# ScalarE in place of GpSimd issues the key copies of the last two attention jobs, and VectorE splits one downward tile sooner

## The chip, the cores and the metric

The program runs on one core of one Trainium2 chip. The metric is device microseconds of one execution (us), lower is better. The kernel before was timed three times: 1089.26, 1090.0 and 1090.44 us, median 1090.0.

PE is TensorE, DVE is VectorE, ACT is ScalarE, POOL is GpSimd and SP is SyncE, which issues the loads. Times inside the profiled execution are us from the start of its span.

## What is computed

One layer of a streaming encoder, batch 1, 512 positions, width 1024, in float32. With `cond = silu(c)` and nine vectors of shift, scale and gate from `cond @ w_ada + b_ada`:

```
h = modulate(x, g_ffn1, shift0, scale0); x = x + 0.5*gate0*swiglu(h, w_ffn1_up, w_ffn1_down)
h = modulate(x, g_mix, shift1, scale1);  proj = h @ w_in     # 8 stick-breaking + 8 forgetting heads of 64
o_sb = rmsnorm(stick_breaking_attention(sb_q, sb_k, sb_v))
o_fx = rmsnorm(forgetting_attention(rmsnorm(fx_q), rmsnorm(fx_k), fx_v, cumsum(log_f))) * sigmoid(fox_gate)
x = x + gate1 * (concat(o_sb, o_fx) @ w_out)
h = modulate(x, g_ffn2, shift2, scale2); x = x + 0.5*gate2*swiglu(h, w_ffn2_up, w_ffn2_down)
return rmsnorm(x, g_final)
```

`swiglu(h, u, d)` is `(silu(gate) * up) @ d`, with gate and up the two halves of `h @ u`; the hidden width is 2816.

## The kernel before

**Products of two halves.** Every float32 operand of a product is kept as a high part in the rounded type float32r and a low part, the rest. A product is three passes on PE (lines 887 to 889, in `three`): high by high, high by low, low by high. So each weight tile of 128x1024 that SP loads (line 763) goes through two steps before PE may use it: ACT writes its high part, DVE subtracts it to get the low part. SP may load the tile that is four later only when DVE has done the low part of the tile in that slot (`load_w` waits on `w_lo_done`).

**Attention jobs.** The 16 heads are worked on in pairs, as eight jobs: 0 to 3 are stick-breaking, 4 to 7 forgetting heads. A job has five units of scores, numbered 0 to 4 below. The order of all work of this stage is one list, `STEPS`, which `mixer_steps` writes in Python from a pattern of letters, some lags and a few steps moved by hand (`AHEAD`). Each engine walks through the same list and does its own share of every step, so an engine never overtakes the list. The steps named below:

- `scores(j, u)`: PE multiplies queries by `k_hh` (line 1194) and `k_l` (line 1195) and adds a mask (line 1196).
- `prep(j, u)`: for forgetting heads DVE subtracts the decay and takes the maximum (line 2415) and negates it (line 2421), then ACT takes the exponential (line 1787). `sum` is DVE's scaling (lines 2444, 2448).
- `turn(j, u)`: PE transposes (line 1218). `unload(j, u)`: ACT copies the high part `pt_hi` (line 1801), DVE subtracts to `pt_lo` (line 2455). `values(j, h)`: PE multiplies by v.
- `square`, `stat`, `scale`, `part`: the norm of a q, k or output chunk. `square` is ACT's line 1730, `stat` PE's line 1246 and ACT's lines 1737 and 1739, `scale` DVE's 2367 and 2372. `part` of a k writes `k_hh` on ACT (line 1757, two halves of 64 partitions) and `k_l` on DVE (line 2390).
- `decay(j, h)`: PE's line 1255 and ACT's line 1765. `evac` of a gate chunk: DVE copies it out (line 2344), ACT takes its sigmoid in three passes (lines 1702, 1704, 1706).

**The copies of k.** Scores need the high part of k on both halves of the partitions. After `part` has written the two halves of `k_hh[j % 2]`, POOL copies each to the other 64 partitions with a DMA from SBUF to SBUF (`repeat_k`, lines 673 and 675, 128 KB each). They count up `k_twice[j % 2]`, and `scores(j, 0)` on PE waits for it. Then POOL issues the next pieces of a set of weight sums that it makes in DRAM for the second FFN (`one_piece`, lines 701 and 703, 1280 KB each, one in flight at a time). SP reads them when the second FFN begins (line 850).

In the list around jobs 6 and 7 the order is:

```
split(93) part(k6) unload(5,2) scores(5,4) prep(5,4) decay(6,0) ... values(5,0) ... decay(6,1) unload(5,3)
scores(6,0) stat(11) prep(6,0) turn(5,4) prep(6,1) scale sum(6,0) unload(5,4) part(q7) scores(6,1) proj turn(6,0) values(5,1)
split(95) part(k7) unload(6,2) scores(6,4) prep(6,4) decay(7,0) ... values(6,0) evac(g6) ... decay(7,1) unload(6,3)
scores(7,0) prep(7,0) ... scores(7,1) ... values(6,1) evac(g7) square(14) ... unload(7,0) scores(7,2) stat(14)
```

**From the up half to the down half of the second FFN.** The hidden chunks (22 of 128x512) are split into high (ACT, line 1522) and low parts (DVE, line 2066, `hidden2_low`). The down weights come in tiles of two chunks of rows, except the third and fourth, which have one each:

```
NAT_PARTS = ((0, 2), (2, 2), (4, 1), (5, 1)) + tuple((k, 2) for k in range(6, 22, 2))
```

A tile passes DVE (`gated`, line 1922, times the gate), ACT (`split_down`, line 1421, high part) and DVE (`split_down_lo`, line 1929, low part). ACT may write the high part of tile n only when PE has finished tile n - 2, since there are two buffers. PE then does tile after tile in order. The order on DVE is written out by hand: low parts of hidden chunks 4 and 5, `gated` of tiles 2 and 3 (counted from 0), chunks 6 to 16, `gated` of tile 4, chunks 17 to 21, and then in turn low part of tile 2, `gated` 5, low part of tile 3, `gated` 6, low part of tile 4, `gated` 7, and so on. Chunk 4 is all that tile 2 (the third) multiplies.

Of the kernel before, what the change touches and what calls it, by code (L numbers as in the profile page):

```python
# [7 lines left out]
F32 = mybir.dt.float32  # L8
# [5 lines left out]
P = 128  # L14
# [6 lines left out]
HD = 64  # L21
# [24 lines left out]
T_DOWN2 = T_UP2 + 2 * SEVEN0 + 4 * (FC - SEVEN0)  # L46
# [5 lines left out]
SPLIT = 2  # L52
# [248 lines left out]
def hybrid_block_kernel(  # L301
# [4 lines left out]
    with ctx:  # L306
        def sem(name):
            return ctx.enter_context(nc.semaphore(name))
# [14 lines left out]
        def keep(name, shape, dt=F32):  # L323
# [103 lines left out]
        k_hh, k_l = (k_hh_a, k_hh_b), (k_l_a, k_l_b)  # L427
# [53 lines left out]
        silu_done, hid_f32, hid_hi_done, hid_done = (  # L481
            sem("silu_done"), sem("hid_f32"), sem("hid_hi_done"), sem("hid_done"))
        mix_zero, k_zero = sem("mix_zero"), sem("k_zero")
        k_twice = [sem("k_twice0"), sem("k_twice1")]
        wf_split, wf_split_hi, f_logit, f_sum, f_act, f_dve = (
            sem("wf_split"), sem("wf_split_hi"), sem("f_logit"), sem("f_sum"), sem("f_act"), sem("f_dve"))
# [154 lines left out]
        def _(pool):  # L641
# [28 lines left out]
            def repeat_k(j):  # L670

                pool.wait_ge(*k_made(j))
                g.dma_start(k_hh[j % 2][HD:P, 0, :].bitcast(F32), k_hh[j % 2][0:HD, 0, :].bitcast(F32))\
                    .then_inc(k_twice[j % 2], 16)
                g.dma_start(k_hh[j % 2][0:HD, 1, :].bitcast(F32), k_hh[j % 2][HD:P, 1, :].bitcast(F32))\
                    .then_inc(k_twice[j % 2], 16)
# [59 lines left out]
                if n == 0:  # L736
                    repeat_k(0)
            for j in range(1, JOBS):
                repeat_k(j)
                if j in (1, 2):  # L740
                    for r in (2 * j - 2, 2 * j - 1):
                        one_piece(sums_rows(S1, r), pieces_rows(up_b, r), True)
                    one_piece(sums_rows(S4, j + 1), pieces_rows(gate_b, j + 1), False)
                elif j == 3:
                    for r in range(3):
                        one_piece(sums_rows(S3, r), pieces_rows(up_a, r), True)
                elif j == 4:
                    one_piece(sums_rows(S3, 3), pieces_rows(up_a, 3), True)
                    one_piece(sums_rows(S2, 0), sums_rows(S1, 0), True)
                elif j == 5:  # L750
                    for r in range(1, 4):
                        one_piece(sums_rows(S2, r), sums_rows(S1, r), True)
                else:
                    for r in (2 * j - 12, 2 * j - 11):
                        one_piece(sums_rows(S4, r), sums_rows(S2, r), True)
# [126 lines left out]
        def _(pe):  # L882
# [167 lines left out]
            for n in range(KC - 1):  # L1050
                pe.wait_ge(x_upd, n + KC - 1)
                for part, (k0, nk) in enumerate(DOWN_PARTS):
                    t = T_DOWN1 + 3 * n + part
# [7 lines left out]
            n = KC - 1  # L1061
            side_bank = (bank[1][:, 0:HALF], bank[3][:, 0:HALF])
            pe.wait_ge(x_upd, n + KC - 1)
            t = T_DOWN1 + 3 * n
# [61 lines left out]
            for step in STEPS:  # L1126
# [49 lines left out]
                elif kind == "scores":  # L1176
                    _, j, u = step
                    unit = 5 * j + u
                    if u == 0:

                        if j == 0:
                            pe.wait_ge(k_zero, 4)
                        pe.wait_ge(k_twice[j % 2], 32 * (j // 2 + 1))
                        if j < SBJ:
                            pe.wait_ge(qk_ready, 2 * j + 2)
                        else:
                            pe.wait_ge(nrm_lo, norm_of("k", j) + 1)
# [210 lines left out]
        def _(act):  # L1398
# [266 lines left out]
            for step in STEPS:  # L1665
# [53 lines left out]
                elif kind == "square":  # L1719
                    m = step[1]  # L1720
                    what, n, ci = NORMS[m]
                    if what == "o":
                        act.wait_ge(pv_done, 2 * n + 2)
                    else:
                        act.wait_ge(w_used, CHUNKS[ci][3] + 1)
                    if m:
                        act.wait_ge(stat_done, stats)
                    else:
                        act.wait_ge(f_dve, 4)
                    a(ssum[:], bank[6 if what == "o" else CHUNKS[ci][2]][:], ACT.Square).then_inc(nsq_done, 1)  # L1730
                elif kind == "stat":
                    m = step[1]
                    stats += 1
                    act.wait_ge(stat_done, stats)
                    if m:
                        act.wait_ge(nrm_f32, m)
                    a(rstd[:], bank[7][:], ACT.Ln, bias=EPS).then_inc(stat_read, 1)
                    act.wait_ge(stat_read, stats)
                    a(rstd[:], rstd[:], ACT.Exp, scale=-0.5).then_inc(nrstd_done, 1)
                elif kind == "part":  # L1740
                    m = step[1]
                    what, n, ci = NORMS[m]
                    if what == "o":
                        if n >= SBJ:
                            act.wait_ge(nrm_gated, n - SBJ + 1)
                        else:
                            act.wait_ge(nrm_f32, m + 1)
                        a(o_hi[:, n, :], nrm[:], ACT.Copy, scale=col(R_GO + n)).then_inc(nrm_hi, 1)
                    else:
                        act.wait_ge(nrm_f32, m + 1)  # L1750
                        act.wait_ge(s_done, 5 * (n - 1))
                        for h in range(2):
                            rows = slice(h * HD, (h + 1) * HD)
                            if what == "q":
                                last = a(q_st[rows, n % 2, h, :], nrm[rows, :], ACT.Copy, scale=gq8[rows, :])
                            else:
                                last = a(k_hh[n % 2][rows, h, :], nrm[rows, :], ACT.Copy, scale=col(R_GK)[rows, :])
                        last.then_inc(nrm_hi, 1)
                elif kind == "decay":
                    _, j, h = step  # L1760
                    stats += 1
                    act.wait_ge(stat_done, stats)
                    if j > SBJ:
                        act.wait_ge(*z_read(5 * j - 1))
                    a(f_keys[:, h, :], bank[7][:], ACT.Copy).then_inc(stat_read, 1)
                elif kind == "prep" and step[1] < SBJ:

                    unit = 5 * step[1] + step[2]
                    buf = tmp_a[:, unit % 2, :]
                    act.wait_ge(s_done, unit + 1)  # L1770
                    if unit >= 2:
                        act.wait_ge(scan_done, unit - 1)
                    a(buf, bank[2 + unit % 2][:], ACT.Abs).then_inc(abs_done, 1)
                    act.wait_ge(abs_done, unit + 1)
                    a(buf, buf, ACT.Exp, scale=-1.0).then_inc(eneg_done, 1)
                    act.wait_ge(eneg_done, unit + 1)
                    a(buf, buf, ACT.Ln, bias=1.0).then_inc(e_ready, 1)
                elif kind == "prep":

                    _, j, u = step  # L1780
                    unit = 5 * j + u
                    buf = tmp_b[:, unit % 2, :]
                    fx = unit - 5 * SBJ
                    act.wait_ge(zf_ready, fx + 1)
                    for s, (h, i, c0) in enumerate(UNITS[u]):
                        seg = buf[:, c0:c0 + (i + 1) * P]
                        last = a(seg, seg, ACT.Exp, bias=small[:, 4 * (unit % 2) + s:4 * (unit % 2) + s + 1],
                                 accum_out=small[:, 8 + 4 * (unit % 2) + s:9 + 4 * (unit % 2) + s])
                    last.then_inc(exp_done, 1)
                elif kind == "exp" and step[1] < SBJ:  # L1790
                    unit = 5 * step[1] + step[2]
                    act.wait_ge(d_ready, unit + 1)
                    a(tmp_b[:, unit % 2, :], tmp_b[:, unit % 2, :], ACT.Exp).then_inc(p_ready_sb, 1)
                elif kind == "unload":
                    _, j, u = step
                    unit = 5 * j + u
                    act.wait_ge(t_done, unit + 1)
                    for h, dst, src in turned(u):
                        if j:
                            act.wait_ge(pv_done, 2 * (j - 1) + h + 1)  # L1800
                        last = a(pt_hi[:, h, dst, :], blocks(bank[4 + unit % 2], src), ACT.Copy)
                    last.then_inc(pt_hi_done, 1)
# [101 lines left out]
        def _(dve):  # L1904
# [654 lines left out]
            for chunk in range(4, FC):  # L2559
                hidden2_low(chunk)  # L2560
                if chunk == 5:
                    gated(2)
                    gated(3)
                elif chunk == 16:
                    gated(4)

            for t in range(T_DOWN2 + SPLIT, T_DOWN2 + len(NAT_PARTS) + SPLIT):
                split_down_lo(t)
                gated(t - T_DOWN2 + 3)
            for tb in range(TB):  # L2570

# [39 lines left out]
```

## Time and profile before

| what | value |
|---|---|
| median of 3 runs | 1090.0 us |
| the profiled execution's own time | 1089.68 us |
| its span in the trace | 1087.9 us |
| granted clock of TensorE | 0.999 of full speed |
| PE busy | 1070.9 us, 98% of the span |
| DVE, ACT, POOL busy | 64%, 46%, 4% |
| chain that ended last | PE 89%, DVE 4%, DMA 2%, ACT 2%, issue 1% |

The span is the time from the first to the last record of the trace; the execution's own time holds 1.8 us around it. PEld is the loading of weights into TensorE, ahead of the matmul that uses them. In a row of a timeline the number in brackets is how long the engine was idle before the row, and the arrow names what it waited for. The first number is the start, the second the duration of all that the row holds.

### The profile page before, as it was taken

How to read it: one execution, taken by the hardware profiler on the slowest of the kernel's cores; microseconds unless marked ns; L12 is line 12 of the kernel's file. 1: busy time of each engine (PE TensorE's matmuls, PEld its weight loads, DVE VectorE, ACT ScalarE, POOL GpSimd, SP SyncE). 2: the span in 40 equal slices, each digit the busy share in tenths (PEclk: the TensorE clock that was granted, in tenths of full speed). 3: DMA queues.
4: the chain of work that ended last, by engine and by line, in shares of the span. 5: the costliest groups of instructions: out<-in, count | busy, mean ns of one | idle time of the engine just before them, and what ended most of it. 6: DMA issues, size and time to landing. Idle time of an engine off the chain costs nothing.

```text
span 1087.9 us, 16282 instructions
## 1 busy us (share of the span) xinstructions
PE 1070.9 (98%) x6072; PEld 911.4 (84%) x6072; DVE 691.8 (64%) x1054; ACT 500.9 (46%) x833; POOL 42.3 (4%) x76
## 2 busy tenths in 40 slices
PE   8999999999999999999999999999999999999997
PEld 5788888888878889888778777789999999978886
DVE  3755555555653557886786676678766667684343
ACT  5523222223222235776796776358544454541222
POOL 1000000000000001110111011000000000000000
PEclk9999999999999999999999999999999999999999
DMA  9868888885474552398699567246777667132221
GB/s 344 239 211 292 264 276 283 275 306 156 140 228 130 176 157 79 90 221 203 142 187 197 124 145 165 77 125 156 190 200 193 171 181 203 60 106 98 87 97 78
DMA packets 209053, 191.84 MB, mean 176 GB/s; under 512 B 7660, under 2 KB 183900, under 8 KB 206940
## 3 DMA queue, kind: packets, MB, share of 16 engines
q1 hardware_dynamic: 201392, 146.86, 45.8%
q0 software_dynamic: 7424, 44.04, 16.1%
q8 instruction: 42, 0.69, 0.3%
q14 instruction: 23, 0.19, 0.1%
q10 hardware_dynamic: 172, 0.06, 0.0%
HBM read 186.74 MB, written 44.04 MB: 212 GB/s over the span
## 4 chain that ended last, share of the span: by engine, by line
PE 89%; DVE 4%; DMA 2%; ACT 2%; issue 1%; SPq 0%; DVEq 0%; POOL 0%; ACTq 0%
PE bank L887 27%; PE bank L889 27%; PE bank L888 27%; PE bank L1246 1%; PE bank L898 1%; PE bank L1218 1%; DVE hid_lo L2066 1%; PE bank L1194 1%; PE bank L1195 1%; DMA x_nat<-in_x_dram 1%; DMA k_hh_b<-k_hh_b 0%; PE bank L924 0%; ACT w_hi L1411 0%; DMA k_hh_a<-k_hh_a 0%; DVE y L2584 0%
## 5 line engine op out<-in xcount | busy, mean ns | idle before, releaser
L887 PE MATMUL bank<-h_hi,w_hi 128*128 128x512 f32 (+1 forms) x592 | 230.3, 389 | 0.1
L889 PE MATMUL bank<-h_hi,w_lo 128*128 128x512 f32 (+1 forms) x592 | 223.5, 378 | 0.0
L888 PE MATMUL bank<-h_lo,w_hi 128*128 128x512 f32 (+1 forms) x592 | 223.5, 378 | 0.0
L1912 DVE TENSOR_TENSOR w_lo<-w_raw,w_hi 128x1024 fp32r<-128x1024 f32 x97 | 118.7, 1225 | 156.1 <-ACT w_hi L1411 155.5
L1411 ACT ACTIVATE w_hi<-w_raw 128x1024 fp32r<-128x1024 f32 x97 | 102.5, 1058 | 204.0 <-PE bank L889 179.2
L887 PEld LDWEIGHTS bank<-h_hi,w_hi 128*128 128x128 f32 x592 | 111.8, 189 | 25.5 <-issue 4.2
L888 PEld LDWEIGHTS bank<-h_lo,w_hi 128*128 128x128 f32 x592 | 111.7, 189 | 24.0 <-issue 2.9
L889 PEld LDWEIGHTS bank<-h_hi,w_lo 128*128 128x128 f32 x592 | 111.6, 189 | 22.6
L2018 DVE TENSOR_TENSOR up_lo<-up_raw,up_hi 128x1024 fp32r<-128x1024 f32 x80 | 86.6, 1085 | 21.1 <-ACT up_hi L1480 21.1
L889 PE MATMUL bank<-combo,up_lo 128*128 128x256 f32 x320 | 90.6, 283 | 0.0
L887 PE MATMUL bank<-combo,up_hi 128*128 128x256 f32 x320 | 90.6, 283 | 0.0
L888 PE MATMUL bank<-combo,up_hi 128*128 128x256 f32 x320 | 90.2, 282 | 0.0
L1480 ACT ACTIVATE up_hi<-up_raw 128x1024 fp32r<-128x1024 f32 x80 | 75.2, 943 | 0.0
L887 PE MATMUL bank<-hid_hi,w_hi 128*128 128x512 f32 (+1 forms) x198 | 74.0, 374 | 1.0 <-DVE w_lo L1912 1.0
L889 PE MATMUL bank<-hid_hi,w_lo 128*128 128x512 f32 (+1 forms) x198 | 73.5, 371 | 0.0
L888 PE MATMUL bank<-hid_lo,w_hi 128*128 128x512 f32 (+1 forms) x198 | 73.4, 371 | 0.0
L889 PE MATMUL bank<-w_hi,hid_lo 128*128 128x512 f32 x176 | 69.8, 396 | 0.0
L887 PE MATMUL bank<-h_hi,up_hi 128*128 128x256 f32 x240 | 68.0, 283 | 0.0
L888 PE MATMUL bank<-h_lo,up_hi 128*128 128x256 f32 x240 | 67.7, 282 | 0.0
L889 PE MATMUL bank<-h_hi,up_lo 128*128 128x256 f32 x240 | 67.6, 282 | 0.0
L1421 ACT ACTIVATE w_hi<-down_raw 128x1024 fp32r<-128x1024 f32 (+1 forms) x24 | 23.7, 987 | 86.6 <-PE bank L889 82.0
L1941 DVE SCALAR_TENSOR_TENSOR ada_acc<-ada_w,cond,ada_acc 128x1024 f32<-128x1024 f32 x49 | 62.6, 1278 | 0.0
(274 smaller groups left out, 2173.5 us busy)
## 6 DMA issues: line engine op xcount, KB each, us to landing
w_sums<-in_w_ffn_up_dram POOLq DMA_DIRECT2D x24, 1280.0 KB, 8.9
ada_w<-in_w_ada_dram SPq DMA_DIRECT2D x56, 512.0 KB, 3.8
w_raw<-in_w_ffn_up_dram SPq DMA_DIRECT2D x48, 512.0 KB, 7.2
up_raw<-w_sums SPq DMA_DIRECT2D x40, 512.0 KB, 5.5
w_raw<-in_w_in_dram SPq DMA_DIRECT2D x28, 512.0 KB, 3.8
w_sums<-w_sums POOLq DMA_DIRECT2D x8, 1280.0 KB, 10.3
up_raw<-in_w_ffn_up_dram SPq DMA_DIRECT2D x20, 512.0 KB, 4.1
down_raw<-in_w_ffn_down_dram SPq DMA_DIRECT2D x20, 512.0 KB, 3.7
```

What stands on the lines that cost most here:

```text
L887: mm(dst, wh, xh, start=start, stop=False, skip_group_check=skip)
L888: mm(dst, wh, xl, start=False, stop=False, skip_group_check=skip)
L889: return mm(dst, wl, xh, start=False, stop=stop, skip_group_check=skip)
L898: last = mm(bank[4 + p][:], cond[:, k:k + 1].broadcast_to([P, P]), ada_first[:, p, k, :], start=k == 0, stop=k == KC - 1)
L1194: mm(zb[:, c0:c0 + n], qs, k_hh[j % 2][:, h, 0:n], start=True, stop=False)
L1195: mm(zb[:, c0:c0 + n], qs, k_l[j % 2][:, h, 0:n], start=False, stop=False)
L1411: a(w_hi[:, s, :], w_raw[:, r, :], ACT.Copy).then_inc(w_hi_done, 1)
L1421: a(w_hi[:, t % SPLIT, 0:n], down_raw[:, t % RAW, 0:n], ACT.Copy).then_inc(w_hi_done, 1)
L1480: a(up_hi[f % 2][q][:], up_raw[n % 3][q][:], ACT.Copy).then_inc(w_hi_done, 1)
L1912: v.tensor_tensor(w_lo[:, s, :], w_raw[:, r, :], w_hi[:, s, :].bitcast(F32), ALU.subtract)\
L1941: ins = v.scalar_tensor_tensor(ada_acc[:], source, cond[:, k:k + 1], ada_acc[:], ALU.mult, ALU.add)
L2018: v.tensor_tensor(up_lo[s][q][:], up_raw[s][q][:], up_hi[f % 2][q][:].bitcast(F32), ALU.subtract)\
```

## The change

Copies of k for jobs 6 and 7 are issued by ACT, right behind the ACT instructions that write `k_hh`, after a wait for their completion. They count up new semaphores, `k_again`, for which PE waits in those jobs. POOL no longer issues them; at its place in these two jobs it waits until they have landed, before it issues the next pieces of the sums. And on DVE the low part of down tile 2 is made after hidden chunk 11 instead of after chunk 21.

```diff
+        k_again = [sem("k_again0"), sem("k_again1")]
...
             for j in range(1, JOBS):
-                repeat_k(j)
+                if j < 6:
+                    repeat_k(j)
+                else:
+                    pool.wait_ge(k_again[j % 2], 32)
...
-                        pe.wait_ge(k_twice[j % 2], 32 * (j // 2 + 1))
+                        pe.wait_ge(*((k_twice[j % 2], 32 * (j // 2 + 1)) if j < 6 else (k_again[j % 2], 32)))
...
                         last.then_inc(nrm_hi, 1)
+                        if what == "k" and n >= 6:
+                            act.wait_ge(*k_made(n))
+                            act.dma_start(k_hh[n % 2][HD:P, 0, :].bitcast(F32), k_hh[n % 2][0:HD, 0, :].bitcast(F32))\
+                                .then_inc(k_again[n % 2], 16)
+                            act.dma_start(k_hh[n % 2][0:HD, 1, :].bitcast(F32), k_hh[n % 2][HD:P, 1, :].bitcast(F32))\
+                                .then_inc(k_again[n % 2], 16)
...
                 if chunk == 5:
                     gated(2)
                     gated(3)
+                elif chunk == 11:
+                    split_down_lo(T_DOWN2 + SPLIT)
                 elif chunk == 16:
                     gated(4)
 
             for t in range(T_DOWN2 + SPLIT, T_DOWN2 + len(NAT_PARTS) + SPLIT):
-                split_down_lo(t)
+                if t > T_DOWN2 + SPLIT:
+                    split_down_lo(t)
                 gated(t - T_DOWN2 + 3)
```

## Rows read from the trace of the kernel before

**Rows 1.** Waits of PE over the whole span: total us, times, longest.
```profile
PE bank L887 <- DVE w_lo L1929: 1.6, 2, 1.3
PE bank L1194 <- DMA k_hh_b<-k_hh_b: 1.3, 1, 1.3
PE bank L1194 <- DMA k_hh_a<-k_hh_a: 1.0, 1, 1.0
```

**Rows 2.** Timeline of all engines around the copies of job 6: start, us, engine.
```profile
626.89 0.66 ACT L1801 ACTIVATE pt_hi<-bank 128x256 fp32r<-128x256 f32 x2
626.90 1.51 DVE L2390 SCALAR_TENSOR_TENSOR k_l_a<-nrm,vcol,k_hh_a 64x512 fp32r<-64x512 f32 x2
...
627.16 0.57 POOL L673 DMA_DIRECT2D k_hh_a<-k_hh_a  x1 [21.56 <-ACT k_hh_a L1757]
...
627.71 0.54 POOL L675 DMA_DIRECT2D k_hh_a<-k_hh_a  x1
...
628.44 0.76 DVE L2455 TENSOR_TENSOR pt_lo<-bank,pt_hi 128x256 fp32r<-128x256 f32 x2
...
632.88 0.49 PE L1194 MATMUL bank<-k_hh_a,q_st 128*128 128x512 f32 x1 [1.01 <-DMA k_hh_a<-k_hh_a]
```

**Rows 3.** Chain of waits, jobs 6 and 7: start and length of the second copy.
```profile
627.71 5.12 DMA k_hh_a<-k_hh_a
...
653.82 5.38 DMA k_hh_b<-k_hh_b
```

**Rows 4.** Timeline: DMA issues of ACT at the start, one of SP beside job 6.
```profile
1.04 0.59 ACTq L1427 DMA_DIRECT2D vecs<-in_c_dram  x1
1.67 0.34 ACTq L1427 DMA_DIRECT2D vecs<-in_b_ada_dram  x1
```
```profile
626.97 0.38 SPq L763 DMA_DIRECT2D w_raw<-in_w_out_dram  x1
```

**Rows 5.** DMA issues, windows 434 to 436 and 553 to 555: median us to landing.
```profile
k_hh_a<-k_hh_a POOLq DMA_DIRECT2D x2, 128.0 KB, 2.5
```
```profile
k_hh_a<-k_hh_a POOLq DMA_DIRECT2D x2, 128.0 KB, 8.9
```

**Rows 6.** Timelines of POOL and SP: last piece of the sums, first reads of them.
```profile
666.64 0.88 POOL L701 DMA_DIRECT2D w_sums<-w_sums  x1 [11.30 <-DMA w_sums<-w_sums]
```
```profile
725.62 1.66 SPq L850 DMA_DIRECT2D up_raw<-w_sums  x2
```

**Rows 7.** Timeline behind scores(6,0).
```profile
634.59 0.68 DVE L2415 CUSTOM_DVE_ANT_0 tmp_b<-bank,f_keys 128x512 f32<-128x512 f32 x1
...
635.79 0.56 DVE L2415 CUSTOM_DVE_ANT_0 tmp_b<-bank,f_keys 128x384 f32<-128x384 f32 x1 [0.32 <-PE bank L1196]
...
639.16 0.19 PEld L887 LDWEIGHTS bank<-pt_hi,v_hi 128*128 128x128 f32 x1 [0.35 <-DVE pt_lo L2455]
```

**Rows 8.** Timeline of PE and ACT behind scores(7,0).
```profile
659.25 0.50 PE L1194 MATMUL bank<-k_hh_b,q_st 128*128 128x512 f32 x1 [1.27 <-DMA k_hh_b<-k_hh_b]
```
```profile
667.76 0.64 ACT L1702 ACTIVATE sig<-sig 128x512 f32<-128x512 f32 x1 [0.65 <-DVE sig L2344]
...
669.63 0.58 ACT L1730 ACTIVATE ssum<-bank 128x512 f32<-128x512 f32 x1
```

**Rows 9.** Timelines of DVE, ACT and PE at the first down tiles.
```profile
957.66 6.70 DVE L2066 TENSOR_TENSOR hid_lo<-hid,hid_hi_b 128x512 fp32r<-128x512 f32 x11
...
968.43 0.68 DVE L1929 TENSOR_TENSOR w_lo<-down_raw,w_hi 128x512 fp32r<-128x512 f32 x1
...
972.95 1.22 DVE L1922 TENSOR_TENSOR down_raw<-down_raw,tmp_b 128x1024 f32<-128x1024 f32 x1 [2.11 <-DMA down_raw<-in_w_ffn_down_dram]
```
```profile
962.38 0.63 ACT L1421 ACTIVATE w_hi<-down_raw 128x512 fp32r<-128x512 f32 x1 [2.30 <-PE bank L889]
```
```profile
969.16 0.50 PE L887 MATMUL bank<-w_hi,hid_hi_b 128*128 128x512 f32 x1 [1.27 <-DVE w_lo L1929]
...
975.37 0.50 PE L887 MATMUL bank<-w_hi,hid_hi_b 128*128 128x512 f32 x1 [0.34 <-DVE w_lo L1929]
```

## The prediction

> **What bounds the kernel now.** PE does. I read the page first: PE is busy 98% of the span and makes up 89% of the chain that ended last, so only a wait of PE is worth anything. The second view is therefore the list of PE's waits [rows 1]. Two of its entries are the copies of k for jobs 6 and 7, 1.0 and 1.3 us, and one is the low part of down tiles, 1.6 us in two waits. The two edits aim at these: 3.9 us at most, 0.36% of the time. The third view is the timeline around each wait, to see what stands right behind it; there most of the 3.9 us goes again. About 0.2% (2.2 us) is what a measurement of this kernel can tell from no change.
>
> **Copies of k: when they can start.** ACT has written k_hh at 626.87, just before its next instruction starts at 626.89; POOL's first issue starts only at 627.16 and its second at 627.71 [rows 2]. ACT can start at about 626.95 (0.05 us for the wait on its own result, my guess from the 0.02 to 0.05 us between dependent rows). How long ACT takes to issue a DMA is shown only at the start of the kernel: 0.34 us for 72 rows, 0.59 us for the first of all [rows 4]. The copies have 64 rows each, so I take 0.34. The second copy is then issued at 627.3 instead of 627.71, 0.4 us sooner, and the same in job 7.
>
> **When they land.** Before, the second copy took 5.12 and 5.38 us [rows 3]. The same copy from POOL took 2.5 us in job 0, with nothing beside it, and 8.9 us in job 4 [rows 5]. Those are the bounds. The nearest rows are those of jobs 6 and 7 themselves: SP issues a load of w_out at 626.97, beside the copies [rows 4], and still will. What goes is POOL's 0.54 us of issue, against ACT's 0.34 [rows 2, 4], and the piece of the sums that POOL issued behind the copies, because POOL now waits for them. I take 4.7 us: landing at 632.0 instead of 632.83, and some 1.1 us sooner in job 7 (4.7 against 5.38, and 0.4 from the start). The Trainium skill, page DMA: Bandwidth & Descriptors, section Issuing engines are not separate DMA queues, says that all issuing engines feed the same 16 DMA engines and another one saves only sequencer time. By that the landing would be only 0.4 us sooner in each job, and the gain below 0.3 + 0.4 instead of 0.3 + 0.65 us; no run so far shows such a copy from ACT.
>
> **What ACT pays.** Behind the copies ACT has unload(5,2), its pt_hi at 626.89 for 0.66 us, done at 627.55. DVE takes it up only at 628.44, since k_l holds DVE from 626.90 to 628.41 [rows 2]. So pt_hi may be 0.86 us late for nothing. The two issues and the wait are 0.05 + 2 x 0.34, and about 0.05 to get going: 0.8 us. I count 0.05 us per job. By the long issue of rows 4 it would be 0.1 + 2 x 0.59 = 1.3 us, so 0.4 us late per job. After pt_hi ACT waits for DVE for about 2.5 us, so nothing else of ACT is touched.
>
> **What POOL pays.** In job 6 its piece goes out about 3 us later, and so do the pieces behind it. The last was issued at 666.64, and SP's first read of the sums is at 725.62 [rows 6]. Nearly 50 us cover it, less the roughly 10 us that a piece takes. Cost 0.
>
> **What is late next, job 6.** PE's 1.01 us before scores(6,0) can go. But DVE's prep(6,0) at 634.59 starts with no wait on PE, since DVE and ACT are behind with their own work, and it won't move. Only prep(6,1), which waited 0.32 us for PE's scores, can come sooner [rows 7]. Its exponential on ACT, then pt_hi and pt_lo of unload(5,4) and PE's values(5,1) at 639.16 hang on it; there PE already waited 0.35 us for DVE [rows 7]. So PE, 1 us ahead, waits there about 0.7 us longer: of 1.01 us, 0.32 stay.
>
> **Job 7.** PE's 1.27 us go [rows 8]. Behind it ACT's and DVE's preps again run on their own time. ACT waits 0.65 us for the gate copy that DVE makes once PE is done with it, then does three passes for the sigmoid and square(14) at 669.63, without a gap [rows 8]. PE's stat(14) waits for that square. ACT's work before the 0.65 us does not move, so square(14) and with it PE can come at most 0.65 us sooner. Of 1.27, 0.65 stay. Sum of the copies: -0.32 - 0.65 + 2 x 0.05 = -0.87 us.
>
> **The down tile.** From 957.66 DVE does chunk after chunk at 6.70 / 11 = 0.61 us, 0.60 from start to start. Chunk 11 is the sixth of this row, so its end is 957.66 + 6 x 0.60 = 961.27. But ACT's high part of tile 2 is there only at 962.38 + 0.63 = 963.01, because it waits for PE to finish tile 0 [rows 9]. DVE, put there, stands still for 1.75 us, with the ten other chunks, gated 4 and 5 and the low part of tile 3 queued behind. The low part of tile 2 is then done at 963.7, and PE's wait of 1.27 us goes: it starts tile 2 at 967.9 instead of 969.16. But DVE ends chunk 21 at 968.43 + 1.75 + 0.60 = 970.8 and needs 1.13 for gated 5 and 0.68 for the low part of tile 3, to 972.6. Tiles 2 and 3 took PE from 969.16 to 975.37 - 0.34 = 975.03, so 2.94 each. PE is through tile 2 at 970.85, waits 1.8 us, starts tile 3 at 972.65 and is through at 975.6. Tile 4 started at 975.37 before. DVE does gated 6 (its load is now there 5 us sooner, so the 2.11 us wait for the DMA goes) and the low part of tile 4 by 972.5 + 1.15 + 1.2 = 974.9 (both steps at the 1.22 us of the 1024-wide row), in time. PE starts tile 4 at 975.6: **0.2 us later than before**. The wait is moved, not removed. Bounds: nothing from these rows could make it better than the 1.61 us of both waits; for the worse, another 0.3 us if DVE is a little slower.
>
> **Sum.** -0.87 + 0.2 = -0.7 us. The profiled execution took 1089.68 us, 1.8 more than its span, 0.3 less than the median of 1090.0; against the median I get 1089.3.
>
> **The rivals.** (a) *PE keeps all that it wins at the copies*: -1.01 - 1.27 + 0.2 = -2.1, so 1087.9. For it: the waits are PE's own, on the chain. Against: the two later waits named above stand in the rows, 0.35 and 0.65 us [rows 7, 8]. (b) *Both edits give in full*: -3.9, so 1086.1. It needs DVE not to stand still at chunk 11, against the 963.01 of rows 9. (c) *ACT issues slowly*, at 0.59 us each: SP issues its load at the same moment [rows 4], and if ACT has to wait for SP, pt_hi is 0.4 us late per job, the whole row of DVE and ACT work behind it too, and the gain of the copies shrinks from 0.97 to 0.2: 1090.0. The Trainium skill, page Perfetto Trace Analysis, section DMA Instruction — HWDGE (DVE, Sync), says that the descriptor generator is shared between sequencers and locked for exclusive use, which speaks for (c). Against (c): at the start of the kernel SP was issuing too, and ACT's second DMA already took only 0.34 us [rows 4]. (d) *The copies land later than before*: it decides from 5.5 us after ACT's second issue on (632.83 - 627.3). The mechanism is the load of w_out, which now goes out at the same moment as the copies and may be served first. At 6.8 us, half way between 4.7 and the 8.9 of job 4 [rows 5], PE waits 1.3 us longer per job: +2.6 + 0.2, so 1092.8. Against: job 4 had a piece of the sums in flight ahead of the copies in the same queue, and here the queue of ACT is empty. (e) *The change of the issuing engine does nothing for PE*, since the landing hangs on the load alone: only the +0.2 of the down tile is left, 1090.2.
>
> **How the numbers follow.** My forecast 0.56; (a) 0.11, (b) 0.04, (c) 0.14, (d) 0.06, (e) 0.09. The forecast, (c) and (e) lie within 0.2% of 1090.0 (1087.8 to 1092.2), (a) just inside, and I give half of it to the other side. Faster by over 0.2%: (b) and half of (a), 0.10. Slower: (d), 0.05. Within: 0.85. For the range I take in (a) at the low end, 1087.7, and (c) and (e) at the high end with the 0.4 us by which runs of one kernel lie above their median, 1090.7. Left out are (b), (d) and the tails, about 0.17.
>
> **What would show it.** In the changed profile: two DMA rows on ACT's queue behind k_hh, 0.3 to 0.4 us each; no wait of PE at line 1194; but a longer wait at values(5,1) for pt_lo, near 1 us, and a new one of 0.6 us at stat(14) for ACT's square. At the down tiles DVE idle for 1.7 us before the low part of tile 2, for ACT; PE's 1.27 us before tile 2 gone and 1.8 us before tile 3 in its place; the 0.34 us before tile 4 gone. I am wrong if PE still waits at line 1194, if ACT's issues are 0.6 us, or if PE starts tile 3 without a wait.

## The result, and the profile after the change

The changed kernel takes **1091.67 us** (median of 20 runs, 1090.17 to 1093.11), the kernel before on the same chip 1089.67 us (20 runs, 1088.66 to 1092.51). The ratio is 1.0013, with a 95% interval of 1.0007 to 1.0019: slower, but by less than the 0.2% that the prediction took as telling a change from none. The 1089.3 us of the prediction and its range up to 1090.7 missed. The profiled execution took 1092.31 us: span 1090.5, granted clock 0.997 (before: 1087.9 and 0.999).

The waits of PE in the changed kernel (total us, times, longest), to be held against [rows 1]. PE's and ACT's lines are 4 further down than before, DVE's 10.

```profile
PE bank L891 <- DVE w_lo L1939: 2.0, 1, 2.0
PE bank L891 <- DVE w_lo L1922: 1.4, 2, 0.9
PE bank L891 <- DVE pt_lo L2465: 0.9, 2, 0.6
...
PE bank L1198 <- DMA k_hh_b<-k_hh_b: 0.5, 1, 0.5
PE bank L1250 <- ACT f_keys L1775: 0.4, 1, 0.4
...
PE bank L1198 <- DMA k_hh_a<-k_hh_a: 0.3, 1, 0.3
```

The waits on the copies did shrink, from 1.0 and 1.3 us to 0.3 and 0.5. In their place stand two waits for `pt_lo`, the low part of the transposed block (0.9 us), and one for `f_keys` (0.4). The down tiles have one wait of 2.0 us instead of two of 1.6 in all. All of PE's waits in this view make 10.5 us, against 10.0 before, only 0.5 us more; a list of waits does not show at what clock PE works. That is the second half of the loss, below.

The timeline of the changed kernel around the copies of job 6, against [rows 2, 4]:

```profile
627.05 0.53 ACTq L1765 DMA_DIRECT2D k_hh_a<-k_hh_a  x1
...
627.12 0.39 SPq L767 DMA_DIRECT2D w_raw<-in_w_out_dram  x1
...
627.61 0.88 ACTq L1767 DMA_DIRECT2D k_hh_a<-k_hh_a  x1
...
628.59 0.66 ACT L1811 ACTIVATE pt_hi<-bank 128x256 fp32r<-128x256 f32 x2 [1.57 <-issue]
...
629.28 0.76 DVE L2465 TENSOR_TENSOR pt_lo<-bank,pt_hi 128x256 fp32r<-128x256 f32 x2 [0.72 <-ACT pt_hi L1811]
...
630.09 0.50 PE L891 MATMUL bank<-pt_hi,v_hi 128*128 128x512 f32 x1 [0.34 <-DVE pt_lo L2465]
```

ACT issues for 0.53 and 0.88 us, in job 7 for 0.49 and 1.14, where I had taken 0.34 each. ACT does no work for 1.57 us ahead of `pt_hi`, and DVE, which was to find it ready, stands still for 0.72 us. The chain of waits of the changed kernel goes the same way (start, us, what):

```profile
627.05 0.53 ACTq L1765
627.61 0.88 ACTq L1767
628.59 0.67 ACT pt_hi L1811 x2
...
629.62 0.41 DVE pt_lo L2465
...
631.68 0.49 ACT f_keys L1775
```
```profile
654.25 5.82 DMA k_hh_b<-k_hh_b
```

In job 6 the chain does not pass through a copy at all: it is ACT's two issues, then PT, then `f_keys`. In job 7 it is the copy again, 5.82 us against the 5.38 of [rows 3].

Now the down tiles, in the timelines of DVE, ACT and PE, against [rows 9]:

```profile
963.99 0.69 DVE L1939 TENSOR_TENSOR w_lo<-down_raw,w_hi 128x512 fp32r<-128x512 f32 x1 [1.70 <-ACT w_hi L1425]
...
972.89 0.69 DVE L1939 TENSOR_TENSOR w_lo<-down_raw,w_hi 128x512 fp32r<-128x512 f32 x1
```
```profile
963.32 0.63 ACT L1425 ACTIVATE w_hi<-down_raw 128x512 fp32r<-128x512 f32 x1 [2.30 <-PE bank L893]
```
```profile
973.63 0.50 PE L891 MATMUL bank<-w_hi,hid_hi_b 128*128 128x512 f32 x1 [2.00 <-DVE w_lo L1939]
973.97 0.40 PE L892 MATMUL bank<-w_lo,hid_hi_b 128*128 128x512 f32 x1
...
975.69 0.63 PE L892 MATMUL bank<-w_lo,hid_hi_b 128*128 128x512 f32 x1
976.12 0.63 PE L893 MATMUL bank<-w_hi,hid_lo 128*128 128x512 f32 x1
```

The waits are the forecast ones: DVE stands still for 1.70 us, and PE's wait is moved from before tile 2 to before tile 3. But then the matmuls change their pace, from one each 0.23 to 0.24 us to one each 0.43. The windows of this stretch say why. A row has start and end, its length, the busy time of PE, PEld, DVE, ACT and POOL with the number of instructions, then the granted clock, the DMA share and GB/s:

```profile
972.00:973.50 1.50, 0.00 (x0) 0.00 (x0) 1.50 (x3) 0.78 (x1) 0.00 (x0) 1.00 0.00 0
973.50:975.00 1.50, 1.37 (x6) 1.14 (x7) 1.50 (x3) 0.00 (x0) 0.00 (x0) 0.99 0.14 30
975.00:976.50 1.50, 1.50 (x5) 1.16 (x4) 0.84 (x1) 0.00 (x0) 0.00 (x0) 0.50 0.78 294
976.50:978.00 1.50, 1.50 (x5) 1.16 (x4) 0.71 (x1) 0.00 (x0) 0.00 (x0) 0.50 0.55 191
978.00:979.50 1.50, 1.50 (x8) 1.17 (x7) 0.81 (x2) 1.06 (x1) 0.00 (x0) 0.87 0.49 184
```

PE is idle, works for 1.4 us at full clock, and is then granted **half of it, 1.2 instead of 2.4 GHz, for 3.4 us**. In the profile before, the clock was 1.00 all through this stretch, as in this row around tile 4:

```profile
975.00:976.50 1.50, 1.16 (x6) 0.95 (x6) 1.31 (x2) 1.06 (x1) 0.00 (x0) 1.00 0.02 1
```

Summed over the windows of the changed kernel, 1.7 us of full clock are missing.

PE's starts, before and after, give the account. The matmul of `f_cum` ahead of job 6 starts at 625.87 and 626.03, the output projection's first waiting matmul at 701.88 and 702.78: the copies cost 0.74 us. Tile 2 starts at 969.16 and 968.66, tile 3 at 972.06 and 973.63, tile 4 at 975.37 and 977.82: 1.55 us lost behind 701.88, and 0.2 more by the time the clock is back. Before the copies the two traces are 0.16 apart. So 0.2 + 0.7 + 1.7 make the 2.6 us between the spans.

### The profile page after: what moved, and what is told of

Its sections match the earlier page's. It is cut to its first block, busy times and chain, and to the rows that moved or that the text cites. A ratio compares the mean times of both kernels' runs of the same rounds, so it can differ in the third digit from the quotient of the medians.

```text
span 1090.5 us, 16284 instructions
## 1 busy us (share of the span) xinstructions
PE 1073.0 (98%) x6072; PEld 912.4 (84%) x6072; DVE 692.2 (63%) x1054; ACT 500.9 (46%) x833; POOL 40.0 (4%) x72
## 4 chain that ended last, share of the span: by engine, by line
PE 89%; DVE 4%; ACT 3%; DMA 2%; issue 1%; ACTq 0%; SPq 0%; DVEq 0%
PE bank L891 27%; PE bank L893 27%; PE bank L892 27%; PE bank L1250 1%; PE bank L902 1%; PE bank L1222 1%; PE bank L1198 1%; DMA w_raw<-in_w_ffn_down_dram 1%; PE bank L1199 1%; DMA x_nat<-in_x_dram 1%; PE bank L1285 1%; ACT w_hi L1415 1%; DMA k_hh_b<-k_hh_b 1%; DVE hid_lo L2076 1%; PE bank L928 0%
```

## The experiments

Twelve kernels ran in three groups (e1 to e4, e5 to e8, e9 to e12), each on another chip. So each ratio is against the kernel before on its own chip. Beside times I read two stretches of each profile, from starts of the same matmuls of PE: **jobs 6 and 7** (`f_cum` at 625.87 to the output projection at 701.88, 76.01 us before), and **down tiles** (from there to tile 4 at 975.37, 273.49 us before). The ratio is not the quotient of the two medians beside it; the two differ by up to 0.11% (e5: 1.0009 by the medians).

| kernel | median, its chip's before | ratio, 95% interval | jobs 6, 7 | down tiles |
|---|---|---|---|---|
| before | | | 76.01 | 273.49 |
| the change | 1091.67, 1089.67 | 1.0013 (1.0007-1.0019) | 76.75 | 275.04 |
| e1 copies only | 1091.19, 1090.85 | 1.0000 (0.9989-1.0010) | 76.80 | 273.49 |
| e2 tile only | 1092.25, 1090.85 | 1.0005 (0.9995-1.0015) | 78.00 | 275.12 |
| e3 tile at chunk 16 | 1088.90, 1090.85 | 0.9979 (0.9970-0.9988) | 76.50 | 271.92 |
| e4 GpSimd copies, SP holds | 1089.87, 1090.85 | 0.9987 (0.9979-0.9996) | 75.13 | 273.83 |
| e5 ACT copies, SP just behind | 1090.82, 1089.82 | 1.0020 (1.0010-1.0030) | 76.17 | 273.83 |
| e6 ACT copies, SP holds | 1090.48, 1089.82 | 1.0008 (1.0000-1.0017) | 76.16 | 273.86 |
| e7 ACT copies late | 1090.35, 1089.82 | 0.9999 (0.9991-1.0008) | 75.75 | 273.50 |
| e8 e4 and e3 | 1087.23, 1089.82 | 0.9976 (0.9966-0.9986) | 75.16 | 271.94 |
| e9 tile at chunk 13 | 1089.03, 1090.91 | 0.9990 (0.9981-1.0000) | 75.76 | 272.54 |
| e10 the change, tile at 16 | 1089.00, 1090.91 | 0.9985 (0.9975-0.9994) | 76.53 | 271.97 |
| e11 as e2 | 1092.14, 1090.91 | 1.0007 (0.9996-1.0018) | 76.59 | 275.29 |
| e12 as e4 | 1089.83, 1090.91 | 0.9995 (0.9986-1.0004) | 75.17 | 273.75 |

### The two edits apart

**e1** has the change's edits of the copies, without the line on DVE; **e2** has only that line. **e3** has it at another place, behind chunk 16 and its pieces:

```diff
                 elif chunk == 16:
                     gated(4)
+                    split_down_lo(T_DOWN2 + SPLIT)
```
**e4** leaves the copies with POOL and holds SP's two loads of w_out beside them until the copies have landed:

```diff
-            with sp.Fori(0, KC // RAW) as i:
-                for j in range(RAW):
-                    load_w(T_OUT + RAW * i + j, j, tile8(w_raw, j), out_v[:, :, bass.ds((RAW * i + j) * P, P)])
+            for n in range(KC):
+                if n == 1:
+                    sp.wait_ge(w_lo_done, T_OUT + n - RAW + 1)
+                    sp.wait_ge(k_twice[0], 128)
+                if n == 3:
+                    sp.wait_ge(w_lo_done, T_OUT + n - RAW + 1)
+                    sp.wait_ge(k_twice[1], 128)
+                load_w(T_OUT + n, n % RAW, tile8(w_raw, n % RAW), out_v[:, :, n * P:(n + 1) * P])
```

> The copies of k for jobs 6 and 7 from ACT, the down tile as before. Theory A (ACT's issues are long, and pt_hi behind them is late): as in the changed kernel, pt_hi of unload(5,2) and unload(6,2) starts about 1.6 us after k_hh, PE waits 0.3 to 0.6 us for pt_lo and still 0.3 to 0.5 us for the copies, and everything after attention is 0.7 us later than before: +0.7 us. No drop of the granted clock near the down tiles, and PE waits 1.27 and 0.34 us there as before. Rival: the copies are worth the forecast -0.9 us and the whole loss is in the down tiles; then this run is 0.9 us below before.

> Only the down tile's low part after chunk 11, the copies on POOL as before. Theory B (the standstill of DVE makes one PE wait of 2.0 us, and behind it the granted clock halves for some 3.3 us): PE starts tile 3 about 0.6 us later than before and is 1.5 us slower in the stretch after it, so up to +1.8 us where the clock falls and +0.2 us where it doesn't; runs lie in two groups 1.6 us apart. Rival: the clock fell in that profile for another reason and has nothing to do with the wait; then this run is +0.2 us with the clock at 1.00 throughout.

> The low part of down tile 2 after hidden chunk 16 and gated 4, where ACT's high part (963.0) has long been there, the copies as before. If the order on DVE alone is what failed: DVE does not stand still, PE starts tile 2 at 967.9 instead of 969.2, tile 3 and tile 4 without a wait, the clock stays at 1.00: -1.5 us against before (1.27 + 0.34 less restarts). Rival (PE's waits there are set by loads or the order of later steps and only move): -0.2 to +0.2 us, with a wait of PE before tile 3 or 4 of over 1 us.

> POOL issues the copies as before, but SP holds the w_out loads of tiles 97 and 99, which went out beside them, until the copies of jobs 6 and 7 have landed. Theory C (the load beside them is what makes the copies take 5.1 and 5.4 us): they land in about 2.6 us as in job 0, PE's waits at the copies go, and by the limits behind them (0.32 and 0.65 us) the kernel is 0.9 to 1.0 us faster. Rival (the piece of the sums behind them, or the path of the copies itself): landing stays at 4.4 us or more, change within 0.3 us of before.

Measured: the copies alone lengthen jobs 6 and 7 to 76.80 us, as the whole change does. The tile alone gives PE's 2.00 us wait before tile 3, half clock behind it, and the slow down tiles of the whole change. So by these stretches both edits lose, and each does it without the other. The times alone do not show it: the median of e2 is 1.4 us above its chip's, that of e1 0.3 us, and neither is clear of no change by its interval.

e3 keeps the idea of the tile and takes the standstill out. Its timeline of DVE:

```profile
960.13 6.70 DVE L2066 TENSOR_TENSOR hid_lo<-hid,hid_hi_b 128x512 fp32r<-128x512 f32 x11
966.76 1.22 DVE L1922 TENSOR_TENSOR down_raw<-down_raw,tmp_b 128x1024 f32<-128x1024 f32 x1
967.89 0.68 DVE L1929 TENSOR_TENSOR w_lo<-down_raw,w_hi 128x512 fp32r<-128x512 f32 x1
968.50 3.09 DVE L2066 TENSOR_TENSOR hid_lo<-hid,hid_hi_b 128x512 fp32r<-128x512 f32 x5
```

DVE never waits for ACT, since `w_hi` is long there at 967.89, and the low part is still done before PE wants it. Both PE waits of [rows 9] are gone (one of 0.2 us is left, before tile 3), the down tiles take 1.6 us less, and the time falls by 0.2%.

e4 shows what the copies are bound by. With SP's load held, PE has no wait on a copy. Jobs 6 and 7 take 75.13 us, 0.88 us less than before and not 2.3, because PE now waits for ACT a little later, once in each job:

```profile
635.77 0.67 PE L1251 MATMUL bank<-ssum,pair_mean 128*128 128x512 f32 x1 [0.98 <-ACT f_keys L1770]
```
```profile
671.77 1.12 PE L1251 MATMUL bank<-ssum,pair_mean 128*128 128x512 f32 x2 [0.79 <-ACT ssum L1735]
```

The first is stat(11), right behind scores(6,0): of PE's 1.0 us in job 6 it leaves 0.1. The second is stat(14), which waits for ACT's square: of job 7's 1.3 us it leaves about 0.65, the limit that the prediction had named.

In the four kernels that hold SP's loads and leave the tile alone (e4, e5, e6, e12) the down tiles take 0.3 to 0.4 us longer than before. It is lost ahead of tile 4, where PE waits 0.55 to 0.69 us (e4, e6, e12) instead of 0.34, and DVE ahead of it 2.33 to 2.46 us for a load of the down weights instead of 2.11. No run separates why.

### Why ACT's copies lose: the issues or the landing

**e5** and **e6** leave the copies with ACT and hold SP's load, e5 only until ACT has done the unload behind its two issues (`sp.wait_ge(pt_hi_done, 28)` and 33), e6 until the copies have landed (`k_again`, 32). **e7** moves ACT's two issues behind `pt_hi` of unload(5,2) and unload(6,2):

```diff
                         last = a(pt_hi[:, h, dst, :], blocks(bank[4 + unit % 2], src), ACT.Copy)
                     last.then_inc(pt_hi_done, 1)
+                    if (j, u) in ((5, 2), (6, 2)):
+                        n = j + 1
+                        act.wait_ge(*k_made(n))
+                        act.dma_start(k_hh[n % 2][HD:P, 0, :].bitcast(F32), k_hh[n % 2][0:HD, 0, :].bitcast(F32))\
+                            .then_inc(k_again[n % 2], 16)
+                        act.dma_start(k_hh[n % 2][0:HD, 1, :].bitcast(F32), k_hh[n % 2][HD:P, 1, :].bitcast(F32))\
+                            .then_inc(k_again[n % 2], 16)
```

> ACT issues the copies for jobs 6 and 7, and the output projection's tile that SP loads beside them (two of them, one per job) is held on SP until ACT has finished the unload that follows its two issues. Theory 1 (ACT's issues are long, 0.53 and 0.88 us for job 6, 0.49 and 1.14 us for job 7, because SP's load of many descriptors is issued at the same moment and shares what makes them): each of the four issues takes 0.35 to 0.5 us, PT's unload starts 0.6 to 0.9 us sooner than with the change, the copies land under 4 us after their issue, and the values matmul group before TensorE's new scores loses no 0.3 us. Theory 2 (the length belongs to an SBUF to SBUF copy issued from ACT): 0.5 and 0.9 to 1.1 us as before, only the landing gets shorter. Time by theory 1 about 1 us below the kernel before, by theory 2 at most 0.5 us below.

> As the run before it, but SP holds its load until both copies of the job have landed, so nothing of SP's lies beside the copies at all. Both theories: landing 2 to 3.5 us after the issue, no wait of TensorE on a copy. Theory 1 (issue length from SP's simultaneous load): issues 0.35 to 0.5 us, the time is that of the kernel in which GpSimd copies and SP holds its load (0.9987 of before), less or more by 0.3 us. Theory 2 (intrinsic length): issues still 0.5 and 0.9 to 1.1 us and TensorE still loses 0.3 to 0.6 us per job on PT's unload, so slower than that kernel by about 1 us.

> ACT issues the copies only after the unload of the last PT unit of the job before (about 0.7 us later than with the change), SP's loads as in the kernel before. If what costs with the change is that the issues stand ahead of PT's unload on ACT, the idle time of ACT ahead of that unload falls from 1.6 to 1.8 us to under 0.7 us, TensorE's values group no longer waits 0.34 to 0.56 us on PT's low part, and the copies land 0.7 to 1.5 us later, so TensorE's wait on them grows from 0.33 and 0.49 us to 1 to 1.6 us: time within 0.5 us of the kernel before. The rival, that the copies are late whoever issues them and wherever, gives the same wait on the copies as the kernel before, 1.0 to 1.7 us, and the same time.

> GpSimd copies, SP holds its load until they have landed: once more, against the kernel in which ACT issues the copies and SP holds as well (1.0008 on another chip, this one 0.9987 on a third). TensorE's times between jobs 5 and 8 showed 0.4 us lost in job 6 and 0.6 us in job 7 by ACT's issues alone, so this kernel should stand about 1 us under that one: 0.9985 to 0.9995. If it is 1.0005 or above, ACT's issues cost nothing and the difference was the chip's.

The timeline of e6 around job 6, where nothing of SP's is issued beside ACT:

```profile
628.24 0.52 ACTq L1770 DMA_DIRECT2D k_hh_a<-k_hh_a  x1
...
628.79 0.60 ACTq L1772 DMA_DIRECT2D k_hh_a<-k_hh_a  x1
...
629.50 0.66 ACT L1816 ACTIVATE pt_hi<-bank 128x256 fp32r<-128x256 f32 x2 [1.29 <-issue]
...
630.19 0.76 DVE L2470 TENSOR_TENSOR pt_lo<-bank,pt_hi 128x256 fp32r<-128x256 f32 x2 [0.44 <-ACT pt_hi L1816]
```

and the same place in e12, where POOL issues:

```profile
627.70 0.66 ACT L1806 ACTIVATE pt_hi<-bank 128x256 fp32r<-128x256 f32 x2
...
627.97 0.57 POOL L673 DMA_DIRECT2D k_hh_a<-k_hh_a  x1 [21.42 <-ACT k_hh_a L1762]
...
628.53 0.54 POOL L675 DMA_DIRECT2D k_hh_a<-k_hh_a  x1
...
629.25 0.76 DVE L2460 TENSOR_TENSOR pt_lo<-bank,pt_hi 128x256 fp32r<-128x256 f32 x2
```

My theory 1, that SP's load makes ACT's issues long, falls for the most part. Without it they take 0.52 and 0.60 us in job 6 and 0.47 and 0.84 in job 7 (e5: 0.60 and 0.88). With it, the second took 0.63 to 0.88 in job 6 (e1, e10 and the change) and 0.87 to 1.20 in job 7, and in e7 0.99 and 0.82, so the load adds 0 to 0.4 us, to the second issue only. That is all the sharing that the Trainium skill's page Perfetto Trace Analysis (section DMA Instruction — HWDGE (DVE, Sync), a descriptor generator locked for exclusive use) could account for here.

The landing is another matter. The views of the DMA issues, job 7 of e6 and of the change (median us to landing; job 6 has 2.3 and 5.1):

```profile
k_hh_b<-k_hh_b ACTq DMA_DIRECT2D x2, 128.0 KB, 2.4
```
```profile
k_hh_b<-k_hh_b ACTq DMA_DIRECT2D x2, 128.0 KB, 5.3
```

The load beside them costs the copies nearly 3 us, whoever issues them (POOL's medians are 4.8 and 4.9 us before, 2.6 and 2.4 in e4). ACT writes `k_hh` 0.16 us later than before in job 6 and 0.73 us later in job 7. Counted from there, it issued the second copy 0.3 us sooner than POOL had, and PE started on it at 633.05 - 0.16 = 632.89 and 660.11 - 0.73 = 659.38, against 632.88 and 659.25 before: **nothing was won**. That is what the Trainium skill's page DMA: Bandwidth & Descriptors, section Issuing engines are not separate DMA queues, leads to (the same 16 DMA engines serve all), and less than I had made of it.

What ACT's issues cost by themselves can be read from the stretch of jobs 6 and 7 in the five kernels in which no copy is late: 75.13, 75.16, 75.17 us where POOL issues, 76.17 and 76.16 where ACT does. **1.0 us for the two jobs**, 0.4 in job 6 and 0.6 in job 7, and these five scatter by only 0.04 us. The theory that it is the issues ahead of `pt_hi` agrees with e7: with them behind it, PE's waits for `pt_lo` are gone and the stretch takes 75.75 us instead of 76.5 to 76.8, though the copies come later and PE again waits 0.67 and 1.11 us for them. Its time is that of the kernel before, as expected. e12 came out at 0.9995, the upper end of what I had expected (0.9985 to 0.9995; 1.0005 would have refuted it); its interval reaches 0.9986 and holds e4's 0.9987. The case for the 1.0 us rests on the stretches, the ratios (e5 and e6 above 1, e4 and e12 below) only agree, on different chips.

One caution: where a copy is late, this stretch scatters. The kernels with POOL's copies and SP's load untouched took 76.01 (before), 76.50 (e3), 75.76 (e9) and 76.59 (e11), mean 76.2 (e2's 78.00 has a half clock in it and is left out); those with ACT's took 76.75, 76.80 and 76.53, mean 76.7. The highest of the first lies above the lowest of the second. So the change's copies cost about 0.5 us by these few profiles; the 0.74 of the first two holds some luck of the landing.

### Why the tile loses: the half clock

**e9** puts the split behind chunk 13 instead of 11, so that ACT is late by less; **e11** is e2 once more. **e10** is the whole change with e3's place for the split, **e8** is e4 and e3 together.

> Only the down tile's edit, but two chunks later: the low part of tile 2 stands after hidden chunk 13. DVE then stands still for about 0.5 us instead of 1.7, and TensorE's wait ahead of tile 3 is about 0.6 us instead of 2.0, with none ahead of tiles 2 and 4. Theory (the size of the wait decides both the tile's cost and whether TensorE's clock is halved behind it): about 1.0 us less than the kernel before, 0.999, and the granted clock stays at 1.00 in the 4 us behind tile 3's start. Rival (the clock falls in this stretch for another reason): a low stretch there all the same, and a time at that of the kernel before or above it.

> The down tile's edit alone once more, for the clock: two profiles had a wait of 2.0 us ahead of tile 3 and 3.3 to 3.5 us of half clock behind it. If the wait brings the half clock every time, it is here a third time, and the time is 1.5 to 2 us above the kernel before on this chip; if it is chance, this profile may have none, and the runs fall in two groups 1.7 us apart.

> The whole change, except that the low part of tile 2 is made after chunk 16 and its pieces instead of after chunk 11. The copies cost what they cost with the change, 0.7 us, and the tiles give 1.6 us, with no half clock behind them: 0.998 to 0.9995 of before, and at least 2 us less than the change itself. If the change were slower mainly for its copies, it would stay at 1.0 or above.

> The two edits that were faster alone, put together: GpSimd copies, SP holds one load per job until they have landed (0.9987 alone), and the low part of the third downward tile of the second FFN is split after chunk 16 and its pieces (0.9979 alone). If their gains are of different waits, they add: 0.996 to 0.998 of before, neither a wait on the copies nor one ahead of tiles 2 and 3. The rival, that each one's gain was only a fast stretch of TensorE's clock regained in some runs, gives 0.998 at best and a PE wait left in the down tiles.

The timeline and windows of e9 behind tile 3's start, then those of e11:

```profile
971.30 0.50 PE L887 MATMUL bank<-w_hi,hid_hi_b 128*128 128x512 f32 x1 [0.80 <-DVE w_lo L1929]
```
```profile
971.50:973.00 1.50, 1.50 (x7) 1.22 (x7) 1.50 (x2) 0.15 (x1) 0.00 (x0) 1.00 0.21 45
973.00:974.50 1.50, 1.50 (x8) 1.19 (x7) 0.51 (x1) 0.04 (x1) 0.00 (x0) 1.00 0.81 292
```
```profile
975.17 0.59 PE L887 MATMUL bank<-w_hi,hid_hi_b 128*128 128x512 f32 x1 [2.01 <-DVE w_lo L1929]
```
```profile
974.50:976.00 1.50, 0.83 (x3) 0.64 (x4) 1.50 (x3) 0.00 (x0) 0.00 (x0) 0.81 0.00 0
976.00:977.50 1.50, 1.50 (x5) 1.21 (x4) 1.39 (x2) 0.00 (x0) 0.00 (x0) 0.50 0.63 157
977.50:979.00 1.50, 1.50 (x5) 1.16 (x5) 0.08 (x1) 0.00 (x0) 0.00 (x0) 0.55 0.79 223
```

With 0.80 us of wait the clock stays at 1.00, and the stretch of the down tiles is 0.95 us shorter than before, the 1.0 us expected. With 2.0 us it fell in each of the three profiles that have the wait (the change, e2, e11). The stretch with the wait and the half clock is 1.55 to 1.8 us longer than before; without the half clock it would be the 0.2 us of the forecast, as tile 3's start shows: 972.06 before and 973.63 after, of which 0.90 us are older (701.88 against 702.78), so 0.67 us late. From that the gap ahead of tile 4 falls away, 0.34 us of idle PE, 0.5 from matmul to matmul. The rest is the clock, 1.4 us up to tile 4 and 1.55 in all: eight matmuls about 0.43 us apart instead of 0.23 to 0.24.

The same happens at places that no edit touched. In the first FFN PE waits for a down tile near 305 us, for a load that is late by more or less; in e3 and in e10 that wait was 1.98 us, and half clock followed, in e3 from 305.5 to 309.0 and in e10 from 306.4 to 309.8. Here are e3's windows, and those of e1, where a wait of 2.01 us had no such effect:

```profile
306.00:309.00 3.00, 3.00 (x8) 2.32 (x7) 1.36 (x3) 1.57 (x2) 0.00 (x0) 0.51 0.42 83
```
```profile
306.00:309.00 3.00, 3.00 (x14) 2.40 (x14) 1.47 (x2) 1.50 (x2) 0.00 (x0) 1.00 0.32 55
```

Of the waits of PE that I looked at in these places, in all profiles, nine are of 1.85 us or more (up to 2.06): seven had half clock behind them, two (1.85 in e2, 2.01 in e1) had not. Of two between 1.6 and 1.7 one had (e2, ahead of scores(6,0), which is why its jobs 6 and 7 took 78.00 us). Of eighteen between 1.0 and 1.52 none had. So a wait near 2 us is a throw of dice for another 1.5 us, by these counts; what decides it is not shown. The Trainium skill's page TensorE: Matmul & The Clock Gate, section HAM oscillation — how this bites in real kernels, describes waits of about 3 to 5 us for a DMA that bring the low clock back in the middle of a kernel. These traces show the same behind single waits of 1.7 to 2.06 us, shorter than the page's, in otherwise full work.

The runs without a trace fall into two groups, which fits: of the change's 20, nine lie between 1090.17 and 1090.94, eleven between 1091.64 and 1093.11, and all seven whose clock is 0.997 are in the upper group. The lower group's median of 1090.69 is 1.0 us above the kernel before: the copies and the tile's 0.2. The upper one's 1092.18 is 1.5 us above that. That it is the down tile's wait which divides the runs is not shown, since only one of them has a trace, and the wait near 305 us can do the same in any of these kernels. But of the 20 runs of the kernel before on this chip only two lie above 1091.6, of the change's eleven.

e10 shows the sum from the other side: the change with the split at chunk 16 is 0.15% faster than before, its down tiles as short as e3's and its copies still at 76.53. And **e8 beats both kernels: 1087.23 us against 1089.82 on its chip, 0.9976**, with runs all within 1.1 us. Its two gains (0.85 us in jobs 6 and 7, 1.55 in the down tiles) add up.

## Why the prediction was wrong, by its steps

- *When the copies can start*: the place was right, the size was not. I took 0.34 us per issue from ACT's second DMA at the start of the kernel [rows 4]. It is 0.5 for the first and 0.6 to 1.2 for the second, with or without SP. Of the price list I had, the 0.59 that I kept for the rival was the better one.
- *When they land*: wrong as well. I let POOL's issue time and the piece of the sums come off the 5.12 and 5.38 us. Neither counted; the load alone sets the landing. Of the expected 0.8 and 1.1 us nothing came.
- *What ACT pays*, **the step that failed**: 0.05 us per job, because `pt_hi` could be 0.86 us late for nothing. The slack was right: `pt_hi` was 1.5 us late (628.59 - 0.16 against 626.89) and the work behind it 0.7. But ACT's hold was 1.57 us and not 0.8, and each bit over the slack goes through pt_lo, DVE's prep, ACT's `f_keys` and PE's statistics in one row. In job 7 the row ends at the square that stat(14) waits for. It costs 0.4 us in job 6 and 0.6 in job 7, not 0.05 (e5, e6 against e4, e8, e12).
- *What POOL pays*: right. Its last piece went out at 670.07 instead of 666.64, still far ahead of SP's first read of the sums at 726.55, and PE waits for none of it.
- *What is late next*: half right. Of the two waits on the copies, 2.3 us, 0.83 to 0.88 could be had (e4, e8, e12), near the 0.97 of my account. Job 7 gave its 0.65 for the reason named, the square that stat(14) waits for (0.79 us in e4). Job 6 gave 0.1 instead of 0.32: I looked for the next wait at values(5,1), and it stood directly behind scores(6,0), at stat(11), for ACT's row up to `f_keys` (0.98 us in e4). That the sum is near is in part luck.
- *The down tile*: the schedule was right to 0.1 us (standstill 1.70 for 1.75, wait 2.0 for 1.8, +0.2 us). What was missing, and so a step that failed too, is that a wait is not only its length. Two waits of 1.27 and 0.34 us had become one of 2.0, and I counted that as equal; the clock behind it did not. The term is +0.2 or +1.7 us.
- *The sum*: -0.87 + 0.2 was forecast; it is +0.5 to +0.7 for the copies, +0.2 for the tile, and in about half of the runs another 1.5. Rival (c), at 1090.0, named the right place, ACT's issue ahead of `pt_hi`, but it kept a gain on the landing that was not there. Rival (e), at 1090.2, had the landing right and left out what ACT pays. The two together make the account of the copies, and no rival had the clock. So nothing reached over 1090.7 but (d), whose mechanism, copies landing later than before, did not come. The copies and the tile without the half clock give the lower group's 1090.69, already slower instead of faster but still at the edge of the range; the half clock is what takes the median out of it. Of the three signs of being wrong that the prediction named, two came: PE still waits at the copies' line, and ACT's issues reach 0.6 us and more.

## What to carry to other kernels

Before a DMA moves to a computing engine's queue, take its issue at 0.5 to 1.2 us of that engine's time, as here, and compare it with the slack of what stands behind it; here the landing came no sooner while a load went beside it. If a small copy is late, hold the load, not the copy: the load had time. And keep TensorE's waits apart: two short ones cost less than one near 2 us, and an instruction that waits for another engine in the middle of a row of work belongs a few places later.

## What was not expected of the hardware

- TensorE's clock fell to half at once (e3, e4) or up to 1.4 us (the change) after a wait near 2 us had ended, and stayed there for 3.4 us each time, while PE was busy without a gap: about 1.5 us lost. It came behind 7 of 9 such waits and behind none of those from 1.0 to 1.52 us.
- A wait is not the only thing that it comes behind. In e7 the clock was also half from 46.1 to 49.5 us, with no wait of PE in the 30 us ahead of it; there PE shows busy all through, but two rows of eight very small matmuls (1x1, 1.05 us, and 128x1, 0.95 us) stand among the large ones. The other 13 profiles have the same work there at full clock. The window of e7:

```profile
46.00:49.50 3.50, 3.50 (x11) 2.67 (x10) 3.40 (x7) 2.83 (x4) 0.00 (x0) 0.51 1.17 307
```

- The second of two equal copies issued back to back by ACT takes longer to issue than the first (0.60 to 0.88 against 0.47 to 0.52 us, with nothing of SP's beside them); the same on POOL takes 0.57 and 0.54.
- Copies of 128 KB from SBUF to SBUF, which ACT issues, land in 2.3 to 2.5 us (e5, e6), POOL's in 2.4 to 2.6 (e4, e8, e12; medians of the two). With a load beside them it is 4.6 to 5.4 us from ACT and 4.8 to 5.0 from POOL, so no gain from ACT shows.
- What stays open: why two of nine long waits had no half clock behind them, and why e5's runs, four of twelve of which lie above 1092.5, are slower than its profile shows, whose run of 1089.96 us is the fastest of them.
